# First projection of a hybrid encoder step: nine pairs of tiles as seven half-size block products

## The chip, the core and the metric

The kernel runs on one core of a Trainium2 chip. The metric is the time of one execution on the device, in microseconds. TensorE multiplies matrices, VectorE, ScalarE and GpSimd do the elementwise work, SyncE issues nearly all transfers between memory and the core's on-chip memory. Each engine runs its own instructions in order; semaphores tie them together.

## The reference

One layer of a streaming encoder is run on 1024 prompt tokens and 32 sample tokens with the same weights. The part that the change touches is the first line and what reads its result:

```python
z = x @ w["w_in"]            # (1056 x 1024) @ (1024 x 6416)
gq, gk, gv, gr, ga, sq, sk, sv, mq, gl = jnp.split(z, SPLIT_AT, axis=-1)
log_a = log_sigmoid(ga @ w["w_gla_a2"] + w["b_gla_a"]) / GLA_TAU
o_a, gla_s = gla_chunked(gq, gk, gv, log_a, gla_s0, ...)   # branch A: recurrence over tokens
q, k = partial_rope(sq, pos), partial_rope(sk, pos)        # branch B: first 16 of 64 dims turned
o_c = mem_attention(mq, mem_k, mem_v)                      # branch C; keys from mem_prompt @ w_mem_kv
g_a, g_b, g_c = jnp.split(sigmoid(gl + w["b_gate"]), 3, axis=-1)
mix = (g_a * y_a + g_b * y_b + g_c * y_c) @ w["w_o"]
x = layer_norm(ALPHA * x + mix);  x = layer_norm(ALPHA * x + conv_ffn(x))
```

All is float32. A product is made of three matmuls on rounded halves: `hi @ hi + hi @ lo + lo @ hi`.

## The kernel before

Activations lie transposed: 128 channels on the partitions, tokens along the free dimension, 1058 columns (1024 prompt, a gap of 2, 32 sample), in three slices of 352, 352 and 354 (`GROUPS`). x arrives as 9 tiles of 128 rows, TensorE turns each (`x_turn`, L1057), ScalarE rounds it to `act_hi` (L1581), VectorE makes the rest, `act_lo` (L2124).

**A dense tile** is 128 columns of `w_in`. SyncE loads it to `w_raw` (`cols`, L564, issued on L562), ScalarE makes `w_hi` (`split_hi`, L1565), VectorE `w_lo` (`split_lo`, L2113). There are two slots; a slot is loaded again when its split is done. TensorE then does three slices (`proj_slice`, L1044) of 8 x 3 matmuls, alternating between banks 0 and 1 of the accumulator. ScalarE copies each slice into `z` (`proj_out`, L1571) or, for a merge gate's tile, into a staging buffer `gate_st` (`gate_out`, L1621), from which SyncE writes it to scratch memory (`gates_scratch`, L619). The count `proj_free` of those copies lets TensorE into a bank again.

**The order of the program.** (1) 16 dense tiles fill `z` (the four inputs of the recurrence); the narrow `ga` (16 columns, L1608 to L1610 and L2147) stands between tiles 14 and 15. (2) The recurrence: 8 steps of 128 tokens and one of 32 (`gla_tile` on each engine). Each step has six places for a slice of a dense tile (`gate_slice`, L1162), so 18 tiles stand beside it: 16 gate tiles (0 to 15), then two of `sq`. (3) Eight more dense tiles (`sk`, `sv`, `sq` 2 and 3, four `mq`), written to the `z` rows that the recurrence has left. After the fourth of them TensorE turns the 256 memory rows (`mem_rows_turn`, L1185), loaded by SyncE on L642 and L643. Beside the last four stand the four tiles of the memory keys (`mem_tile`). Rotary embedding needs rows of `z` moved to other partitions: per tile, four transfers of 8 partitions each (`rope_rows`, L658), a product with `sin` on VectorE (L2218), with `cos` on GpSimd (L897), and a sum (L2222). (4) Attention over window and memory, 8 more gate tiles, the merge of the branches, `w_o`, the first norm. (5) The up-projection of the FFN. (6) The down-projection and the second norm.

**The up-projection is already in block form.** A pair of tiles (256 columns) is cut into 2 x 2 blocks: 512 + 512 input channels, 128 + 128 output columns, and the tokens of a slice in two halves of 256 or 274 (`HALF`). Seven products of half size replace eight. A product is 4 x 3 matmuls (`block_product`, L1438, its matmuls L1462); both token slices follow each other within a product, so a pair has 7 x 2 x 12 = 168 matmuls. GpSimd makes four sums of weight blocks, ScalarE rounds the seven operands (L1886), VectorE makes their low parts (L2449). ScalarE copies four results out of the accumulator (`snap_out`, L1934), VectorE adds three (`combine`, L2492). Sums of x blocks are made once.

## Time and profile before

| | us |
|---|---|
| median of 3 runs | 1777.21 (1776.03 to 1777.63) |
| the profiled execution | 1777.36 |
| its span in the trace | 1775.5 |
| mean granted TensorE clock in it | 0.996 of full speed |

The profile is one execution, with the start and the duration of every instruction on every engine, and what released an engine that had been idle. Copies out of the accumulator mark the progress of the program: the last slice of the second dense tile is copied at 45.0 us, the copies of `ga` begin at 199.44, that of the last slice beside the recurrence is at 476.00. The chain enters the steady part of the up-projection at 1093.46.

### The profile page before, as it was taken

To read this page: it belongs to the slowest core of one execution; us is meant where nothing else is said; L and a number is where in the kernel's file an instruction comes from. 1 tells how busy PE (TensorE), PEld (TensorE's weight loads), DVE (VectorE), ACT (ScalarE), POOL (GpSimd) and SP (SyncE) were. 2 spreads that over 40 slices of the span, in tenths; PEclk is the share of its full clock that TensorE was granted. 3 is DMA by queue.
4 is the path that set the end of the run, shared out by engine and by line. 5 is a ranking of instruction groups with operands and counts; after the bars stand their busy time and mean duration, and the time that the engine had idled before them with its cause. 6 is when DMAs were issued, how large, how long until landed. Compare 5 with 4: busy or idle time off the path is not lost.

```text
span 1775.5 us, 31156 instructions
## 1 busy us (share of the span) xinstructions
PE 1750.6 (99%) x11872; PEld 1695.5 (95%) x11872; DVE 1001.9 (56%) x1379; ACT 716.7 (40%) x1272; POOL 231.7 (13%) x324
## 2 busy tenths in 40 slices
PE   8999999999999999999999999999999999999997
PEld 7999999999999799989998889999999999999997
DVE  3111165555242766657656688777777677554464
ACT  3222244343222555554332245545444454433342
POOL 0000000000020200000000014333333331002011
PEclk9999999999999999999999999999999999999999
DMA  5111122122422411124454232222222223885662
GB/s 176 48 47 36 46 67 84 60 88 66 118 58 72 128 50 48 33 75 136 133 181 143 82 91 74 72 86 81 79 77 72 72 72 107 260 266 165 214 228 73
DMA packets 181451, 180.30 MB, mean 102 GB/s; under 512 B 21021, under 2 KB 149086, under 8 KB 181374
## 3 DMA queue, kind: packets, MB, share of 16 engines
q1 hardware_dynamic: 179518, 173.24, 32.1%
q0 software_dynamic: 1856, 5.99, 0.9%
q8 instruction: 53, 0.87, 0.2%
q14 instruction: 24, 0.20, 0.0%
HBM read 143.08 MB, written 35.53 MB: 101 GB/s over the span
## 4 chain that ended last, share of the span: by engine, by line
PE 94%; DVE 3%; issue 1%; ACT 1%; DMA 1%; POOL 0%; SPq 0%; ACTq 0%; POOLq 0%; DVEq 0%
PE banks L1462 24%; PE banks L1028 19%; PE banks L1029 18%; PE banks L1030 18%; PE banks L1419 5%; PE banks L1256 1%; PE banks L1273 1%; PE banks L1236 1%; PE banks L1268 1%; PE banks L1241 1%; DMA x_rows<-in_x_prompt 0%; PE banks L1136 0%; PE banks L1148 0%; PE banks L1142 0%; PE banks L1430 0%
## 5 line engine op out<-in xcount | busy, mean ns | idle before, releaser
L1028 PE MATMUL banks<-act_hi,w_hi 128*128 128x352 f32 (+1 forms) x1200 | 395.9, 330 | 1.3 <-DVE act_lo L2124 1.3
L1030 PE MATMUL banks<-act_hi,w_lo 128*128 128x352 f32 (+1 forms) x1200 | 390.1, 325 | 0.0
L1029 PE MATMUL banks<-act_lo,w_hi 128*128 128x352 f32 (+1 forms) x1200 | 389.9, 325 | 0.0
L2113 DVE TENSOR_TENSOR w_lo<-w_raw,w_hi 128x1024 fp32r<-128x1024 f32 x70 | 87.3, 1248 | 317.4 <-ACT w_hi L1565 317.4
L1028 PEld LDWEIGHTS banks<-act_hi,w_hi 128*128 128x128 f32 x1200 | 226.9, 189 | 6.1 <-issue 2.4
L1462 PE MATMUL banks<-x_free_r,a_hi 128*128 128x256 f32 x1232 | 226.8, 282 | 0.8 <-DVE a_lo L2449 0.5
L1029 PEld LDWEIGHTS banks<-act_lo,w_hi 128*128 128x128 f32 x1200 | 226.8, 189 | 0.4
L1030 PEld LDWEIGHTS banks<-act_hi,w_lo 128*128 128x128 f32 x1200 | 226.7, 189 | 0.0
L1462 PEld LDWEIGHTS banks<-x_free_r,a_hi 128*128 128x128 f32 x1232 | 190.1, 188 | 1.3 <-DVE x_free_r L2475 0.7
L1462 PE MATMUL banks<-xs_hi,a_hi 128*128 128x274 f32 x616 | 178.8, 290 | 1.7 <-DVE xs_lo L2475 1.0
L1462 PE MATMUL banks<-xs_lo,a_hi 128*128 128x274 f32 x616 | 178.4, 290 | 0.0
L1462 PE MATMUL banks<-xs_hi,a_lo 128*128 128x274 f32 x616 | 178.3, 289 | 0.0
L1462 PE MATMUL banks<-x_free_r,a_lo 128*128 128x256 f32 x616 | 173.4, 281 | 0.0
L1029 PE MATMUL banks<-h_lo,w_hi 128*128 128x384 f32 (+1 forms) x448 | 147.3, 329 | 0.0
L1028 PE MATMUL banks<-h_hi,w_hi 128*128 128x384 f32 (+1 forms) x448 | 146.8, 328 | 0.0
L1030 PE MATMUL banks<-h_hi,w_lo 128*128 128x384 f32 (+1 forms) x448 | 146.5, 327 | 0.0
L1571 ACT ACTIVATE z<-banks 128x352 f32<-128x352 f32 (+3 forms) x78 | 36.4, 466 | 239.3 <-PE banks L1030 239.3
L2605 DVE TENSOR_TENSOR w_lo<-w_raw,w_hi 128x1024 fp32r<-128x1024 f32 x56 | 68.5, 1224 | 93.7 <-ACT w_hi L2044 93.3
L1462 PEld LDWEIGHTS banks<-xs_hi,a_hi 128*128 128x128 f32 x616 | 116.4, 189 | 2.3 <-DVE xs_lo L2475 1.5
L1462 PEld LDWEIGHTS banks<-xs_lo,a_hi 128*128 128x128 f32 x616 | 116.7, 190 | 0.0
L1462 PEld LDWEIGHTS banks<-x_free_r,a_lo 128*128 128x128 f32 x616 | 116.6, 189 | 0.0
L1462 PEld LDWEIGHTS banks<-xs_hi,a_lo 128*128 128x128 f32 x616 | 116.3, 189 | 0.0
(314 smaller groups left out, 3335.2 us busy)
## 6 DMA issues: line engine op xcount, KB each, us to landing
w_raw<-in_w_down SPq DMA_DIRECT2D x112, 256.0 KB, 3.4
w_raw<-in_w_in SPq DMA_DIRECT2D x100, 256.0 KB, 3.3
gate_in<-gates_scratch SPq DMA_DIRECT2D x24, 529.0 KB, 3.8
h_keep<-conv SPq DMA_DIRECT2D x22, 530.0 KB, 2.7
w_raw<-in_w_up SPq DMA_DIRECT2D x44, 256.0 KB, 3.8
x_free<-in_w_up SPq DMA_DIRECT2D x44, 256.0 KB, 3.6
h_raw<-h_keep SPq DMA_DIRECT2D x22, 384.0 KB, 5.1
gates_scratch<-gate_st SPq DMA_DIRECT2D x32, 176.0 KB, 1.9
```

Source lines behind the costliest of these rows:

```text
L1028: pe.matmul(out, hi, b_hi, start=start, stop=False)
L1029: pe.matmul(out, hi, b_lo, start=False, stop=False)
L1030: return pe.matmul(out, lo, b_hi, start=False, stop=stop)
L1236: last = pe.matmul(psum[0:w, 2 + r, h * 256:h * 256 + nk], qs[b][rows_, 2 * u + h, 0:w], keys[rows_, 0:nk], start=True, stop=True)
L1241: last = pe.matmul(out, mqs[b][:, h, 0:w], mkT[mem][:, h, :], start=True, stop=True)
L1256: last = pe.transpose(pair8(4)[0:n, 2 * h + s, 0:w], prob[par][0:w, h, s * P:s * P + n], ident[0:w, 0:w])
L1268: last = pe.matmul(bank4(6)[64 * r:64 * r + 64, h, 0:w], pair_[s][0:n, 64 * r:64 * r + 64], prob_T[0:n, 2 * (2 * r + h) + s, 0:w], start=( ...
L1419: last = pe.matmul(bank(b + half), x[:, k, c:c + P], w[:, place, 512 * half:512 * half + 512], start=k == 0 and n_ == 0, stop=k == KD - 1 ...
L1462: last = pe.matmul(out, a[j][:, k, :], x[s][j][:, k, :], start=fresh and k == 0 and n_ == 0, stop=k == 3 and n_ == 2, skip_group_check=True)
L1571: act.activation(z[:, bass.ds(chunk, 1), c:c + w].rearrange("p k c -> p (k c)"), bank(par)[:, 0:w], ACT.Copy).then_inc(q.proj_free, 1)
L2113: dve.tensor_tensor(dst[:, :, :], w_raw[slot][:, :, :], src[:, :, :].bitcast(F32), ALU.subtract).then_inc(q.w_split_lo, 1)
L2605: dve.tensor_tensor(d_lo[i][:, :, :], d_raw[i][:, :, :], d_hi[i][:, :, :].bitcast(F32), ALU.subtract)\
```

## The change

The first projection gets the block form for nine pairs, 18 of its tiles. In the code of after, `zd` are the staging buffers of two dense tiles, `zt_*` the sums of x blocks and their halves, `za_*` those of the weights, `zu` the staging buffers of a pair, `xf` an unrounded copy of x.

- x is copied once more out of the accumulator to `xf`: five of the nine tiles by ScalarE, three full ones and the one of 32 columns by VectorE.
- Tiles 0 and 1 stay dense. Then come seven pairs (tiles 2 to 15 of `z`) and two pairs of gate tiles (12 to 15). VectorE makes the sums of x and of the weights. Results go to `zu` and from there to scratch memory, since the sums, `zt_*`, lie where `z` is.
- Then gate tile 10, `ga`, gate tile 11, all dense. The constants of `ga` and of the recurrence are loaded here, and `z` is read back in two transfers, 256 columns and the other 802.
- The 18 places beside the recurrence hold `sq` 0 and 1, `sk`, `sv`, `sq` 2 and 3, two `mq`, and gates 0 to 9. All go by the staging buffers to scratch memory.
- After the recurrence two `mq` tiles are left; the memory rows are turned in the second, and the four tiles of memory keys follow in a row.
- Rotary embedding works on the 16 turned rows of each half tile, packed: 30 transfers read them from scratch memory, VectorE does the arithmetic for four tiles at once, 10 transfers write them back. `sq`, `sk`, `sv` and `mq` come back from scratch memory too.

```diff
+        def z_load(n):
+            par = n % 2
+            col = C_GQ + (2 + 2 * n) * P if n < 7 else C_GL + (12 + 2 * (n - 7)) * P
+            for half in range(2):
...
+        def z_keep(n):
+            to = Z_KEEP + 2 + 2 * n if n < 7 else 12 + 2 * (n - 7)
+            for s in range(2):
+                sp.wait_ge(q.combined[s], 3 * n + 3)
+                sp.wait_ge(q.snapped[s], 4 * n + 4)
+            sp.wait_ge(q.z_stored, z_stored_count(n - 1))
+            sp.dma_start(gates[to:to + 2].rearrange("r p c -> p r c"), zu[n % 2][:, :, :]).then_inc(q.z_stored, 16)
...
+        for s in range(2):
+            sp.wait_ge(q.prod_mm[s], ZA)
+        sp.dma_start(wga[:, :, :], w_in[:, :, C_GA:C_GA + RANK]).then_inc(q.gla_consts, 16)
...
+        def z_again(lo, hi):
+            sp.dma_start(z[:, :, lo:hi], gates[Z_KEEP:Z_KEEP + 16, :, lo:hi].rearrange("r p c -> p r c")).then_inc(q.z_back, 16)
+        z_again(0, 2 * P)
+        z_keep(NZ - 1)
...
+        fill_load(0)
+        staged_store(PS_Z, 0, 10)
+        staged_store(PS_Z, 1, 10)
+        sp.wait_ge(q.z_back, 16)
+        z_again(2 * P, TT)
...
-            sp.wait_ge(gate_stored[s], 16 * 16)
+            sp.wait_ge(gate_stored[s], 16 * 20)
         sp.wait_ge(q.st_state, 32)
+        def turned_rows(dst, row, landed):
+            for h in range(2):
+                to, of = ROPE_DIM * h, SWA_HD * h
+                sp.dma_start(dst[0][0][dst[1] + to:dst[1] + to + 16, :], gates[A_KEEP + row, of:of + 16, :]).then_inc(landed, 16)
+                for a, b in ((0, 8), (8, 0)):
+                    sp.dma_start(dst[0][1][dst[1] + to + a:dst[1] + to + a + 8, :], gates[A_KEEP + row, of + b:of + b + 8, :]).then_inc(landed, 16)
+        turned_rows((k_rot, 0), 8, rot_landed[0])
         sp.dma_start(cos[:, :], I["c_cos"]).then_inc(q.att_consts, 16)
         sp.dma_start(sin[:, :], I["c_sin"]).then_inc(q.att_consts, 16)
-        for j in range(2):
-            swa_q(T_ATT // 2 + 2, j, 2 + j)
+        for row in range(4):
+            turned_rows((rot, 32 * row), row, rot_landed[1])
+        sp.dma_start(z[:, 0:6, 6 * P:TT], gates[A_KEEP:A_KEEP + 6, :, 6 * P:TT].rearrange("r p c -> p r c")).then_inc(q.z_back, 16)
...
         sp.dma_start(mem_rows[0][:, :], I["mem_prompt"][0, 0:P, :]).then_inc(q.mem_in, 16)
...
+        def z_product(n, par, s, j):
...
+            for k in range(4):
+                for n_, (a, v) in enumerate(((za_hi, x_hi), (za_hi, x_lo), (za_lo, x_hi))):
+                    last = pe.matmul(bank(b)[:, 0:w], a[j][:, k, :], v[:, k, :], start=fresh and k == 0 and n_ == 0, ...)
...
-        for t in range(9):
-            c, w = tok(t)
...
+        x_out(1, xf)
+        x_out(2, xf)
...
+            if t >= 5:
+                dve.tensor_copy(xf[:, :, c:c + w], x_bank(t)[:, :, 0:w]).then_inc(q.x_lo_done, 1)
...
-        for n_ in range(2, 10):
-            if n_ < 6:
-                turn_, slot = (T_ATT + n_) // 2, n_ % 2
+        for n_ in range(2):
+            tile_start(T_MQ // 2, n_)
...
+        for i in range(4):
+            mem_tile(T_MK // 2 + i // 2, i % 2, 0, i)
```

**ScalarE's list in the first pair.** Here `zd` is the copy of a dense slice, `zt_hi` the rounding of an x sum, `za_hi` that of a weight block, and the first `zu` the copy of the pair's first product. Before, at the second dense tile:

```order
L1571 ACTIVATE z<-banks 128x354 [waits proj_done]
L1565 ACTIVATE w_hi_59<-w_raw_57 128x1024 [waits w_landed0]
L1571 ACTIVATE z<-banks 128x352 [waits proj_done] x2
L1571 ACTIVATE z<-banks 128x354 [waits proj_done]
L1565 ACTIVATE w_hi_60<-w_raw_58 128x1024 [waits w_landed1]
L1597 ACTIVATE prm<-banks 128x289 [waits prm_turned]
```

After, at the same tile:

```order
L1813 ACTIVATE za_hi_111<-z_sum_105 128x512 [waits a_summed]
L1813 ACTIVATE za_hi_114<-z_sum_105 128x512 [waits a_summed]
L1785 ACTIVATE zd_103<-banks 128x352 [waits proj_done]
L1791 ACTIVATE zt_hi_82<-zt_sum_98 128x1096 [waits x_summed]
L1791 ACTIVATE zt_hi_83<-zt_sum_99 128x1096 [waits x_summed]
L1785 ACTIVATE zd_103<-banks 128x354 [waits proj_done]
L1813 ACTIVATE za_hi_113<-z_sum_104 128x512 [waits proj_done,a_summed]
L1813 ACTIVATE za_hi_115<-w_raw_58 128x512 [waits proj_done,w_landed1]
L1827 ACTIVATE zu_106<-banks 128x256 [waits x_summed,prod_mm0]
L1827 ACTIVATE zu_106<-banks 128x256 [waits prod_mm0] x2
```

Between the slices of the second dense tile and behind them there are now six roundings, and the product's copy stands behind them all.

**SyncE's list between the pairs and the recurrence, after.** The rows before the first of these are loads of gate tile 10's and 11's weights; `L617` is the load of a dense tile.

```order
L699 DMA wga<-in_w_in 128x8x16 [waits prod_mm1,prod_mm0]
L700 DMA causal<-in_c_causal 128x128
L702 DMA wa_raw<-in_w_gla_a 16x512 x6
L704 DMA wa_raw<-in_b_gla_a 1x512 x2
L708 DMA z<-gates_scratch 128x16x256
L677 DMA gates_scratch<-zu_106 128x2x1058 [waits snapped1,combined1,z_stored,snapped0,combined0]
L617 DMA w_raw_57<-in_w_in 128x8x64 [waits w_split_lo]
L617 DMA w_raw_57<-in_w_in 128x8x64
L726 DMA gates_scratch<-gate_st_153 128x352 [waits proj_free]
L726 DMA gates_scratch<-gate_st_154 128x352 [waits proj_free]
L708 DMA z<-gates_scratch 128x16x802 [waits z_back]
```

The constants wait for the last product of the pairs, and the next tile's weights stand behind them, behind the first read of `z` and behind the store of the last pair. Before, the constants stood at the start of the program (L598 to L603), and this place held weight loads alone.

**SyncE's list at the end of the recurrence.** Before (the waits on the stores are the same semaphores as after):

```order
L638 DMA cos<-in_c_cos 128x1058 [waits gate_stored1,gate_stored2,gate_stored0,st_state,ds_mm,gla_out]
L639 DMA sin<-in_c_sin 128x1058
L562 DMA w_raw_57<-in_w_in 128x8x64 [waits w_split_lo]
L562 DMA w_raw_57<-in_w_in 128x8x64
L562 DMA w_raw_58<-in_w_in 128x8x64 [waits w_split_lo]
L562 DMA w_raw_58<-in_w_in 128x8x64
L642 DMA mem_rows_125<-in_mem_prompt 128x1024
L643 DMA mem_rows_126<-in_mem_prompt 128x1024
L644 DMA mask<-in_c_mask 128x256
L645 DMA mask_first<-in_c_mask_first 128x256
L658 DMA rot_127<-z 8x1058 [waits proj_free,rot_cleared]
L658 DMA rot_127<-z 8x1058 x3
```

After, where `k_rot` and `rot` hold the packed rows:

```order
L782 DMA k_rot_183<-gates_scratch 16x1058 [waits gate_stored1,gate_stored2,gate_stored0,st_state,ds_mm,gla_out]
L784 DMA k_rot_184<-gates_scratch 8x1058 x2
L782 DMA k_rot_183<-gates_scratch 16x1058
L784 DMA k_rot_184<-gates_scratch 8x1058 x2
L787 DMA cos<-in_c_cos 128x1058
L788 DMA sin<-in_c_sin 128x1058
L782 DMA rot_181<-gates_scratch 16x1058
L784 DMA rot_182<-gates_scratch 8x1058 x2
```

and, after six more groups of three such transfers:

```order
L782 DMA rot_181<-gates_scratch 16x1058
L784 DMA rot_182<-gates_scratch 8x1058 x2
L791 DMA z<-gates_scratch 128x6x290
L792 DMA z<-gates_scratch 128x290
L793 DMA kpad<-gates_scratch 128x1058
L794 DMA mem_rows_179<-in_mem_prompt 128x1024
L795 DMA mem_rows_180<-in_mem_prompt 128x1024
L796 DMA mask<-in_c_mask 128x256
L797 DMA mask_first<-in_c_mask_first 128x256
```

The memory rows and the masks stood behind two constants and four weight loads; now they stand behind 30 row transfers, two constants and three reads.

## Rows read from the trace of the kernel before

**Rows 1.** Page, part 1: each engine's busy time (share of the span) and instructions.
```profile
PE 1750.6 (99%) x11872; PEld 1695.5 (95%) x11872; DVE 1001.9 (56%) x1379; ACT 716.7 (40%) x1272; POOL 231.7 (13%) x324
```

**Rows 2.** Page, part 4, the chain's shares; waits of TensorE: total, times, longest.
```profile
PE 94%; DVE 3%; issue 1%; ACT 1%; DMA 1%; POOL 0%; SPq 0%; ACTq 0%; POOLq 0%; DVEq 0%
...
PE banks L1064 <- DMA x_rows<-in_x_prompt: 3.6, 2, 3.1
```

**Rows 3.** Timeline of ScalarE, dense loop: start, duration, operation [idle before <-releaser].
```profile
57.02 0.47 ACT L1571 ACTIVATE z<-banks 128x354 f32 x1 [3.41 <-PE banks L1030]
...
68.68 0.47 ACT L1571 ACTIVATE z<-banks 128x354 f32 x1 [3.42 <-PE banks L1030]
```

**Rows 4.** Chain that ended last, by time: its longest piece (start, duration, count).
```profile
1093.46 408.10 PE banks L1462 x3312
```

**Rows 5.** Timelines of VectorE, then TensorE, where the third dense slice begins.
```profile
26.39 1.21 DVE L2113 TENSOR_TENSOR w_lo<-w_raw,w_hi 128x1024 fp32r<-128x1024 f32 x1
27.52 1.55 DVE L2124 TENSOR_TENSOR act_lo<-banks,act_hi 128x1024 fp32r<-128x1024 f32 x2
...
29.13 0.44 PE L1028 MATMUL banks<-act_hi,w_hi 128*128 128x354 f32 x1 [0.37 <-DVE act_lo L2124]
```

**Rows 6.** Groups by form (total, mean ns); last, two operations of VectorE's timeline.
```profile
L2492 DVE TENSOR_TENSOR u<-banks,snap 128x256 f32<-128x256 f32 x44 | 18.1, 412 | 2.1 <-PE banks L1462 2.1
L2605 DVE TENSOR_TENSOR d_lo<-d_raw,d_hi 128x1024 fp32r<-128x1024 f32 x10 | 12.2, 1221 | 5.2 <-ACT d_hi L2044 5.1
...
L1886 ACT ACTIVATE a_hi<-w_raw 128x512 fp32r<-128x512 f32 x33 | 20.7, 627 | 21.0 <-PE banks L1462 18.2 <-PE banks L1430 2.8
...
250.37 0.69 DVE L2169 TENSOR_TENSOR e_t<-b_s 128x512 f32<-128x512 f32 x1
250.97 0.69 DVE L2171 SCALAR_TENSOR_TENSOR q_dec<-z,e_p 128x512 f32<-128x512 f32 x1
```

**Rows 7.** SyncE by tile: count, issue time min/median/max in ns, first and last start.
```profile
L658 SPq DMA_DIRECT2D rot<-z x20: 624/625/797, 482.3 to 530.0; - x20
...
L601 SPq DMA_DIRECT2D wa_raw<-in_w_gla_a x6: 419/420/2779, 16.9 to 21.6; - x6
```

**Rows 8.** DMA issues: count, KB each, median us from issue to landing.
```profile
gates_scratch<-gate_st SPq DMA_DIRECT2D x32, 176.0 KB, 1.9
...
mem_rows<-in_mem_prompt SPq DMA_DIRECT2D x2, 512.0 KB, 5.1
```

**Rows 9.** Windows: busy PE, PEld, DVE, ACT, POOL, granted clock, DMA share, GB/s.
```profile
10.00:13.00 3.00, 0.00 (x0) 0.00 (x0) 2.94 (x3) 1.99 (x3) 0.00 (x0) 0.91 1.01 404
13.00:14.50 1.50, 1.41 (x7) 1.41 (x8) 0.54 (x1) 0.00 (x0) 0.00 (x0) 0.50 1.11 332
15.20:16.00 0.80, 0.80 (x5) 0.80 (x4) 0.00 (x0) 0.80 (x1) 0.00 (x0) 0.57 1.09 392
46.00:190.00 144.00, 144.00 (x891) 144.00 (x890) 15.93 (x13) 29.33 (x51) 0.00 (x0) 1.00 0.17 45
1480.00:1560.00 80.00, 80.00 (x514) 80.00 (x514) 49.10 (x52) 37.35 (x47) 5.05 (x12) 1.00 0.62 198
```

**Rows 10.** Timelines of ScalarE, then SyncE, around the end of the recurrence.
```profile
476.00 0.47 ACT L1571 ACTIVATE z<-banks 128x354 f32<-128x354 f32 x1 [3.10 <-PE banks L1030]
...
473.63 0.34 SPq L638 DMA_DIRECT2D cos<-in_c_cos  x1
...
479.73 1.03 SPq L642 DMA_DIRECT2D mem_rows<-in_mem_prompt  x1
```

**Rows 11.** TensorE by tile: the transposes of the memory rows.
```profile
L1185 PE MATMUL banks<-ident,mem_rows x16: 271/273/273, 514.6 to 520.1; 128*128 128x128 f32 x16
```

**Rows 12.** Timelines of ScalarE and VectorE: the three steps of one `ga` slice.
```profile
199.44 0.45 ACT L1608 ACTIVATE ga_T<-banks 32x352 fp32r<-32x352 f32 x1 [1.17 <-PE banks L1097]
...
200.47 0.45 ACT L1610 ACTIVATE ga_T<-banks 32x352 fp32r<-32x352 f32 x1 [0.58 <-DVE ga_T L2147]
...
199.92 0.52 DVE L2147 TENSOR_TENSOR ga_T<-banks,ga_T 32x352 fp32r<-32x352 f32 x1 [0.40 <-ACT ga_T L1608]
```

784 lines of the change are left out of this document (558 added, 226 removed).

## The prediction

> **What bounds the kernel now.** I read the page first: TensorE is busy for 1750.6 of 1775.5 us, VectorE and ScalarE for about half [rows 1], and the chain that ended last is 94% TensorE [rows 2]. So any column of a matmul that goes away is time won, and any wait that TensorE gets is time lost, one for one. The list of who waited for whom gives TensorE under 10 us of waits in the whole span, most of it for the first transfers, so nothing that the other engines do today is paid for. Two unit prices follow. A dense tile (72 matmuls of 352 or 354 columns) takes 11.66 us: the copies of the third slice of two tiles in a row start at 57.02 and 68.68 [rows 3]. A pair of tiles as seven block products (168 matmuls of 256 or 274 columns) is what the up-projection already does: 3312 of them in 408.10 us [rows 4] are 19.71 pairs of 20.70 us, 123 ns a matmul.
>
> **The change part by part.**
>
> *The products.* Nine pairs leave the dense form: 9 x (2 x 11.66 - 20.70) = 23.6 us off the path. The count of tiles stays 42 up to the first scores (2 + 18 + 2 alone, 18 beside the recurrence, 2 for the memory queries). In the steady loop each pair asks VectorE for 11 operations of 512 and 6 of about 265 elements. One of 512 lasts 0.69 and the next begins 0.60 after it when they stand in a row [rows 6], so I take 0.63; one of 1024 lasts 1.21 and lets the next in after 1.13 [rows 5], so 1.19. That is 11 x 0.63 + 6 x 0.41 = 9.4 us, and less on ScalarE, inside 20.7 us. The loads of 1.05 MB and the store of 1.08 MB a pair need 7 us of transfer at 320 GB/s. Cost of those: nothing, the products cover them; without cover 9.4 us a pair.
>
> *The start.* VectorE now also copies four of the tiles into `xf`, three ahead of what the third dense slice waits for, and ScalarE copies five. Before, VectorE's last two `act_lo` operations began at 27.52 and TensorE went on at 29.13 after a wait of 0.37 [rows 5]. Now two full copies of 1.13 us pitch stand between, less what was idle: the third slice starts at about 31.0. Cost 1.9 us (1 to 3).
>
> *The first pair.* VectorE is free of x at 31.3. In front of the fourth weight sum its list holds 12 operations of 1024 or 1096 elements and 8 of 512: 12 x 1.19 + 8 x 0.63 = 19.3 us, so 50.6. ScalarE has the split that waits for this sum in front of two slice copies, two x-sum copies, two splits and only then the copy of the first product (0.55 + 2 x 0.4 + 2 x 1.05 + 2 x 0.5 + 0.4 = 4.9 us; a split of 512 elements lasts 0.63 [rows 6], a tenth less in a row, a slice's copy 0.47 [rows 3]), and 0.3 for the hand-overs: 55.8. TensorE ends the six dense slices at 46.8 and three products later, at 51.1, needs that copy: a wait of 4.7 us. The same list gives two more, 0.4 and 1.5 us, where products 6 wait for `combined` behind splits. Sum 6.6 us (4 to 8).
>
> *From the pairs to the recurrence.* Let T be the end of the ninth pair. Ten small transfers (issue 0.46 us each, rows of `wa_raw` [rows 7]) start only at T, so the constants land at T + 6.6, and ScalarE, which waits for them, frees the first dense slice at T + 8.9; TensorE asked at T + 7.8: 1.2 us. Behind them on the queue stand 2.1 MB (z, 256 columns), 1.1 MB (last store) and 0.5 MB (weights). At full occupation this trace moved 198/0.62 = 320 GB/s, 45/0.17 = 265 for 512-byte pieces, and 404 for rows of 4 KB [rows 9]. With 320 the weights land at T + 4.6 + 11.6 + 2 = T + 18.2. ScalarE's split stands ahead of its `ga_T` copies and VectorE's ahead of its own: 1.05 + 1.22 + 1.4 for the three steps of a slice [rows 12] gives T + 21.9, while TensorE wants the bank for the third `ga` slice at T + 18.0: 3.9 us. The remaining 6.6 MB then need 20.5 us, the second tile of weights lands at about T + 39.5 and ScalarE, stuck behind its split, is free for the first gate of the recurrence at T + 43.7; TensorE needs it at T + 44.9. At 265 GB/s this would be a wait of 4. I take 0.5. The 2.8 MB fetched in the eighth recurrence step delay one weight split by 1 to 2 us against 1.6 of slack: 0.5. Sum 6.1 us (3 to 13).
>
> *From the recurrence to the scores.* Let G be the end of the recurrence's last fill; before, its copy stands at 476.00 [rows 10]. Before, SyncE issued `cos` at 473.63 and the memory rows at 479.73 [rows 10], and TensorE first used them at 514.6 [rows 11]: 35 us of cover. Now the fills are stored, and SyncE must see the last store land first: G + 0.5 + 0.4 + 1.9 [rows 8] = G + 2.8. Ahead of `mem_rows` stand 30 row transfers: 10 of 16 partitions at 0.46 us and 20 of 8 partitions at 0.67 (issue 0.42 and 0.625 plus the gap [rows 7]), 18.0 us, then `cos` and `sin`, 0.8. So the first large transfer goes at G + 21.6. Up to the masks it is 2.9 MB, 8.4 us at 345 GB/s (between 320 and 404, since half of it is rows of 4 KB), and 2 us to land: G + 32. And only two dense tiles are left before the memory products, with the turn of the memory rows after the first slice of the second: G + 11.7 + 3.9 = G + 15.5. TensorE waits 16.5 us. Bounds: all 30 at 0.46 and 404 GB/s give 11; 8-partition issues of 0.8 (the longest row) and 320 GB/s give 20. The four memory tiles now stand in a row, 2.5 us each, and two of them have only one buffer's lead for load and split: 1.5 us more (0 to 3). Rope itself, the `cos` product and the kpad copy were behind cover and stay so. Sum 18.0 us.
>
> The row shows 0.625 us for the issue of an 8-partition transfer and 0.42 for one of 16 [rows 7]. The Trainium skill, DMA: Bandwidth & Descriptors, section Why a DMA increments its semaphore by 16 and not by 1, says that a transfer runs on the largest number of engines up to 16 that divides its outermost dimensions, and that the issuer itself writes the missing increments when it is fewer; the trace agrees with that as a reason for the difference.
>
> *The clock.* After a wait of 3.1 us at the start the granted clock stood at 0.50, the lower level of 1.2 GHz, until about 15.9 [rows 9]: 2.8 us at half speed cost 1.4. Two of the new waits are longer. I add 1.3 for each, 2.6 (0 to 4). The Trainium skill, TensorE: Matmul & The Clock Gate, section Part 1: The HAM clock gate, says that an idle array is throttled to half and is given full speed back after sustained work. By it the long wait costs this; the trace agrees.
>
> **Sum.** -23.6 + 1.9 + 6.6 + 6.1 + 18.0 + 2.6 = +11.6 us. The profiled execution took 1777.4 us (span 1775.5), within 0.2 of the median 1777.2; so 1789.0 us, 0.7% slower. The bounds added up are -4 and +25; a measurement tells 0.2% (3.6 us) from no change.
>
> **The rivals.** *The memory rows are covered after all* (the other side). If the 30 issues overlap with the wait for the last store, or the row transfers and the large reads run side by side at 400 GB/s, the wait at G + 15.5 shrinks to 3 or less with no cold clock: 1789.0 - 13.5 - 1.3 = 1774.2; with the first pair and T at their lower bounds (2.6 and 3.1 less) 1768.5. It decides where the large reads start before G + 6. For it: mask and memory rows landed in 5 us before. Against: all sit on one queue, in order, behind a wait. *The scratch reload is the bound*: 9.8 MB in pieces of 1 to 3 KB at 265 GB/s or less, with fills' stores behind it, adds 4 at the recurrence's first step and 3 at the third `ga` slice: 1796. For: ScalarE stands in order behind weight splits. Against: 320 seen with mixed pieces. *The pairs run slower than in the up-projection*, since VectorE now makes the sums itself: one late `combined` of 0.8 us in each of 9 pairs is 7 us: 1796. Against: VectorE carries more there (the conv and GpSimd beside it).
>
> **Chances.** Forecast 0.55 (1782 to 1796); memory rows covered 0.28, of which 0.16 ends faster by over 0.2% and 0.12 within; reload 0.12; slow pairs 0.05. So faster 0.16, same 0.14 (0.02 of it from the forecast's low end), slower 0.70. Range for 8 in 10: 1773 to 1799.
>
> **What would show it.** Dense pairs gone: 1512 matmuls of the L1462 shape in nine stretches of 20.7 us. TensorE idle before the third product's stretch at 51 us, before the third `ga` slice, and, longest of all, before the first transpose of `mem_rows`, put down to a transfer; on SyncE 18 us of row issues just before. If that last wait is under 5 us, the forecast is wrong in its largest term; if the nine pairs take more than 190 us with no wait named above, the gain is.

## The result, and the profile after

The changed kernel takes 1787.89 us in the median of 5 executions (1785.18 to 1790.10), beside 1777.21 for the kernel before: a ratio of 1.0061, 95% interval 1.0046 to 1.0076. It is slower, by 10.7 us, where 1789.0 was forecast. The profiled execution is the slowest of the five, 1790.1 us with a span of 1788.0; the distances below are measured in it, against the profiled execution of before (1777.4, span 1775.5).

The page of the changed kernel, part 1 and the chain's shares, which answer to [rows 1, 2]:

```profile
PE 1736.7 (97%) x12088; PEld 1679.5 (94%) x12088; DVE 1079.6 (60%) x1529; ACT 749.9 (42%) x1348; POOL 219.2 (12%) x319
...
PE 89%; DVE 5%; DMA 2%; ACT 2%; issue 1%; SPq 1%; POOL 0%; ACTq 0%; POOLq 0%; DVEq 0%
```

TensorE is busy 13.9 us less, and the span is 12.5 us longer. The chain's TensorE share fell from 94 to 89%. The list of TensorE's waits in the changed kernel (engine, tile and line, releaser: total us, times, longest) says on what:

```profile
PE banks L1386 <- DMA mask_first<-in_c_mask_first: 14.9, 1, 14.9
PE banks L1302 <- ACT ga_T L1922: 4.8, 1, 4.8
PE banks L1171 <- DVE act_lo L2422: 3.6, 2, 2.6
...
PE banks L1228 <- ACT zu L1827: 2.3, 1, 2.3
PE banks L1228 <- DVE zu L2473: 1.6, 1, 1.6
PE banks L1171 <- DVE w_lo L2411: 1.2, 1, 1.2
...
PE banks L1171 <- ACT gate_st L1912: 0.9, 1, 0.9
```

In the order of the program: `act_lo` and `w_lo` are the start, the two `zu` are the first pair, `ga_T` and `gate_st` stand between the pairs and the recurrence, and `mask_first` is the wait before the memory rows are transposed. Two pieces of the chain of the changed kernel, in order of time (start, duration, count):

```profile
75.85 166.96 PE banks L1228 x1356
...
1106.53 408.12 PE banks L1659 x3312
```

And the milestones between them: on TensorE's timeline the first product and the first scores,

```profile
50.92 0.28 PE L1228 MATMUL banks<-act_hi,za_hi 128*128 128x256 f32 x1
...
595.74 1.14 PE L1433 MATMUL banks<-ks,qs 64*128 64x256 f32 x8
```

the first scores of the kernel before,

```profile
582.81 1.14 PE L1236 MATMUL banks<-ks,qs 64*128 64x256 f32 x8
```

and on ScalarE's the copy of the last fill's last slice:

```profile
541.50 0.47 ACT L1912 ACTIVATE gate_st<-banks 128x354 f32<-128x354 f32 x1 [3.03 <-PE banks L1173]
```

The long stretch of pairs runs without a stop until 242.81, 123 ns a matmul or 20.7 us a pair, just as the up-projection [rows 4] does. So the gain of the products is there in full, and all that was lost lies in four places. The start of the steady part moved from 1093.46 [rows 4] to 1106.53. By milestones (before: six dense slices end at 45.00, the last fill's copy is at 476.00 [rows 10], the first scores begin at 582.81):

| stretch | cost measured, us | forecast, us |
|---|---|---|
| start, to the first product | +5.9 | +1.9 |
| first pair (50.92 to 77.3, against 20.7) | +5.7 | +6.6 |
| end of pairs (242.81) to the last fill's copy | +7.6 | +6.1 and 1.3 for the clock |
| last fill's copy to the first scores | +17.4 | +18.0 and 1.3 for the clock |
| nine pairs | -23.6 | -23.6 |
| sum at the first scores | +13.0 | +11.6 |

For the third line, before's stretch is 476.00 - 45.00 less 12 dense tiles of 11.66 (the changed kernel makes 18 tiles as pairs ahead of it, and before had six of those behind the last fill): 291.1, against 298.7. For the fourth it is 106.8 less those six, 36.8, against 54.2.

Two of these costs differ from trace to trace, and the trace shown is of the slowest execution. Experiments 1, 2, 3, 5, 6 and 9 below leave everything up to the second pair as it is; there the start and the first pair together cost 8.2 to 10.4 us, against 11.6 here and 8.5 forecast. Experiments 3, 4, 6, 7, 8 and 10 leave everything behind the last fill as it is; there the fourth cost is 13.6 to 17.2.

The longest wait can be read from SyncE's timeline of the changed kernel (start, duration, transfer, count):

```profile
544.01 0.34 SPq L782 DMA_DIRECT2D k_rot<-gates_scratch  x1
...
554.86 0.65 SPq L784 DMA_DIRECT2D rot<-gates_scratch  x2
...
557.04 0.53 SPq L794 DMA_DIRECT2D mem_rows<-in_mem_prompt  x1
...
558.77 0.52 SPq L797 DMA_DIRECT2D mask_first<-in_c_mask_first  x1
```

and from TensorE's, with the idle time before the operation:

```profile
571.93 1.33 PE L1386 MATMUL banks<-ident,mem_rows 128*128 128x128 f32 x5 [14.91 <-DMA mask_first<-in_c_mask_first]
```

With G for the copy at 541.50: the row transfers begin at G + 2.5 and TensorE stops at G + 15.5, both where the prediction has them (2.8 and 15.5). But the rows and the two constants leave the queue after 11.5 us, not 18.8, and the last mask, issued at 558.77, lands 13.2 us later, not 2 us behind 8.4 us of transfer. The two errors nearly cancel. Windows of the changed kernel show what happened in those 13 us (busy PE, PEld, DVE, ACT, POOL, granted clock, DMA share, GB/s):

```profile
550.00:553.00 3.00, 3.00 (x21) 3.00 (x20) 0.45 (x1) 0.00 (x0) 0.00 (x0) 1.00 0.86 167
553.00:556.00 3.00, 3.00 (x20) 3.00 (x19) 2.90 (x3) 0.47 (x1) 0.00 (x0) 1.00 0.68 120
556.00:560.00 4.00, 1.01 (x7) 0.72 (x5) 0.33 (x1) 0.00 (x0) 0.00 (x0) 0.97 0.97 125
...
565.00:570.00 5.00, 0.00 (x0) 0.00 (x0) 2.18 (x2) 0.00 (x0) 0.00 (x0) 0.50 1.04 396
```

From 550 to 560 the DMA engines are 68 to 97% busy and move only 120 to 167 GB/s; the large reads behind the rows move 396. The last column but two is the clock: 0.50 while TensorE stands.

### The profile page after: what moved, and what is told of

Read it like the earlier page. It is cut to its first block, busy times and chain, and to the rows that moved or that the text cites. A ratio compares the mean times of both kernels' runs of the same rounds, so it can differ in the third digit from the quotient of the medians.

```text
span 1788.0 us, 31834 instructions
## 1 busy us (share of the span) xinstructions
PE 1736.7 (97%) x12088; PEld 1679.5 (94%) x12088; DVE 1079.6 (60%) x1529; ACT 749.9 (42%) x1348; POOL 219.2 (12%) x319
## 4 chain that ended last, share of the span: by engine, by line
PE 89%; DVE 5%; DMA 2%; ACT 2%; issue 1%; SPq 1%; POOL 0%; ACTq 0%; POOLq 0%; DVEq 0%
PE banks L1659 23%; PE banks L1171 14%; PE banks L1172 14%; PE banks L1173 13%; PE banks L1228 10%; PE banks L1616 5%; PE banks L1453 1%; PE banks L1470 1%; PE banks L1433 1%; PE banks L1465 1%; PE banks L1438 1%; DMA mask_first<-in_c_mask_first 1%; DMA w_raw<-in_w_in 1%; PE banks L1343 0%; PE banks L1355 0%
## 5 line engine op out<-in xcount | busy, mean ns | idle before, releaser
L1171 PE MATMUL banks<-act_hi,w_hi 128*128 128x352 f32 (+1 forms) x768 | 258.0, 336 | 5.6 <-DVE act_lo L2422 3.6
L1172 PE MATMUL banks<-act_lo,w_hi 128*128 128x352 f32 (+1 forms) x768 | 251.8, 328 | 0.0
L1173 PE MATMUL banks<-act_hi,w_lo 128*128 128x352 f32 (+1 forms) x768 | 251.8, 328 | 0.0
L1171 PEld LDWEIGHTS banks<-act_hi,w_hi 128*128 128x128 f32 x768 | 147.2, 192 | 9.8 <-DVE act_lo L2422 4.2
L1172 PEld LDWEIGHTS banks<-act_lo,w_hi 128*128 128x128 f32 x768 | 147.0, 191 | 0.4
L1173 PEld LDWEIGHTS banks<-act_hi,w_lo 128*128 128x128 f32 x768 | 147.0, 191 | 0.0
L2411 DVE TENSOR_TENSOR w_lo<-w_raw,w_hi 128x1024 fp32r<-128x1024 f32 x52 | 63.7, 1225 | 118.3 <-ACT w_hi L1762 118.3
L3021 DVE TENSOR_TENSOR w_lo<-w_raw,w_hi 128x1024 fp32r<-128x1024 f32 x56 | 68.4, 1223 | 91.8 <-ACT w_hi L2342 91.6
L2865 DVE TENSOR_TENSOR a_lo<-a_sum,a_hi 128x512 fp32r<-128x512 f32 x86 | 83.6, 972 | 40.7 <-ACT a_hi L2184 39.5
```

The lines of the kernel that those rows point to most:

```text
L1171: pe.matmul(out, hi, b_hi, start=start, stop=False)
L1172: pe.matmul(out, hi, b_lo, start=False, stop=False)
L1173: return pe.matmul(out, lo, b_hi, start=False, stop=stop)
L2411: dve.tensor_tensor(dst[:, :, :], w_raw[slot][:, :, :], src[:, :, :].bitcast(F32), ALU.subtract).then_inc(q.w_split_lo, 1)
L2865: dve.tensor_tensor(a_lo[j][:, :, :], src, a_hi[j][:, :, :].bitcast(F32), ALU.subtract).then_inc(q.a_lo_done, 1)
L3021: dve.tensor_tensor(d_lo[i][:, :, :], d_raw[i][:, :, :], d_hi[i][:, :, :].bitcast(F32), ALU.subtract)\
```

## The experiments

My theory after the result: each of the four places is a matter of order. A step sits in an in-order list behind something that it does not need. The rivals: that each wait is transfer time, which another order only shifts; and that behind each wait the next one is already due, so that a repair of one gains little. All kernels below are the changed kernel with one edit, unless said otherwise; times are medians, and gains are against 1787.9.

**1. The memory rows ahead of the row transfers.**

```diff
+        sp.dma_start(mem_rows[0][:, :], I["mem_prompt"][0, 0:P, :]).then_inc(q.mem_in, 16)
...
+        sp.dma_start(mask_first[:, :], I["c_mask_first"]).then_inc(q.mem_in, 16)
         turned_rows((k_rot, 0), 8, rot_landed[0])
```

> The changed kernel, with the four loads of the memory rows and the masks issued ahead of the 30 row transfers of rope instead of behind them; nothing else moves. Theory (the wait of 14.9 us before the first transpose of the memory rows is their place behind 30 issues and three reads): that wait goes to 0, since the rows land about 8 us after the last store. But the weights of the first key tile keep their place behind the rows, and ScalarE's split of them stands ahead of its copy of the last query tile's first slice; in the changed kernel it waited for them until 575.9. So TensorE meets a new wait of about 7 us at the third slice of that tile, and the gain is 8 us and perhaps 1 of clock: about 1779. Rival 1 (the bytes are what takes the time, not the order: 2.9 MB at 340 GB/s must pass in any order): the wait shrinks by 2 us at most, 1786. Rival 2 (the memory rows were the only thing late): the whole 14.9 and the cold clock go, 1771.

Measured: 1784.14 (1779.92 to 1785.27), ratio 1.0035 [1.0021, 1.0049]: 3.8 us gained of 14.9. In this kernel's list of TensorE's waits:

```profile
PE banks L1171 <- ACT z L1768: 12.4, 1, 12.4
```

and ScalarE's timeline:

```profile
570.54 1.06 ACT L1762 ACTIVATE w_hi<-w_raw 128x1024 fp32r<-128x1024 f32 x1 [19.98 <-DMA w_raw<-in_w_mem_kv]
```

The wait for `mask_first` is gone, and one of 12.4 stands a dense tile later. The next thing TensorE needs are the keys' weights, and they still sit behind the 30 rows. ScalarE waits 20 us for them, with the copy that frees TensorE's bank behind it in its list. In the changed kernel that split waited already (at 575.87, idle 22.24), hidden by the wait in front.

**2. The keys' weights ahead as well.**

```diff
+        mem_tile(T_MK // 2, 0, 0, 0)
+        mem_tile(T_MK // 2, 1, 0, 1)
         turned_rows((k_rot, 0), 8, rot_landed[0])
```

> As the run before, and the loads of the first two key tiles stand ahead of the row transfers too. Theory: ScalarE's split is no longer late, so the last query tile runs through; but VectorE's low part of the first key tile stands behind rope in its list, and rope ends some 24 us after the last store, so TensorE waits for it about 3 us, and about 4 for the third key tile, whose load stands behind rope's write-backs. Gain against the changed kernel 14.9 + 2 of clock - 7, about 10: 1778. Rival (rope has slack, as it had before the change): 17 us, 1771. Rival (ScalarE's split was not what held the copies): the same as the run before.

Measured: 1785.0 (1783.56 to 1787.21), ratio 1.0048 [1.0031, 1.0064]. No gain over the first. This kernel's list of TensorE's waits:

```profile
PE banks L1171 <- DVE mem_lo L2651: 13.4, 1, 13.4
```

and ScalarE's timeline:

```profile
572.70 1.94 ACT L1990 ACTIVATE mem_hi<-banks 128x1024 fp32r<-128x1024 f32 x2 [14.12 <-DMA kpad<-k_rot]
```

and the end of VectorE's turn of the keys, and their write-back on SyncE:

```profile
560.52 1.25 DVE L2643 TENSOR_TENSOR k_rot<-k_rot,k_rot 32x1058 f32<-32x1058 f32 x1
...
569.65 1.28 SPq L807 DMA_DIRECT2D kpad<-k_rot  x2
```

This one I had overlooked. `mem_hi` lies where `k_rot` lay, so ScalarE may write it only when the turned keys are written back to `kpad`. VectorE has turned them at 561.8, but SyncE issues the write-back only at 569.65: it stands behind the wait for the large reads of `z` and `kpad`. So a shared buffer hands SyncE's order on to ScalarE.

**3. The recurrence's first weights ahead of `z` and the last store.**

```diff
-        z_again(0, 2 * P)
-        z_keep(NZ - 1)
         fill_load(0)
+        z_again(0, 2 * P)
+        z_keep(NZ - 1)
         staged_store(PS_Z, 0, 10)
```

> The changed kernel, with the load of the first tile beside the recurrence issued ahead of the first read of z and of the last pair's store, instead of behind them. Theory (the wait of 4.8 us at the third ga slice is ScalarE standing in front of a weight load that lies behind 3.2 MB): the load lands about 5 us after the constants instead of 14, the 4.8 us and the half-speed stretch behind it (about 2 us) go, and the reads of z end 1.5 us later, which the recurrence does not feel: 1788 - 6.5 = 1781.5. Rival (z is the bound: what the weights gain, the first step of the recurrence gives back, since its read of z ends later): no change, 1788 within 1.

Measured: 1786.68 (1784.59 to 1788.39), ratio 1.0053 [1.0036, 1.0070]. The split of the weights now starts at 255.05, but the wait for `ga_T` is still 5.1. ScalarE's row:

```profile
264.45 0.45 ACT L1922 ACTIVATE ga_T<-banks 32x352 fp32r<-32x352 f32 x1 [6.72 <-DVE ga_T L2566]
```

The releaser is now VectorE. It stands on its wait for the last pair's store, ahead of the clearing of `att`, and the weight split and its part of `ga_T` come behind. Again a second wait of the same length, one list further on.

**4. The first pair in another order.** The sums for products 3 and 4 go ahead of the second x sums on VectorE, and the combination of the first products ahead of the second half's sums.

```diff
         z_x_sums(1)
-        z_low(0, 0, 2)
-        z_sums34(0, 0)
...
         z_low(0, 0, 1)
+        z_low(0, 0, 2)
+        z_sums34(0, 0)
```

> The changed kernel, with VectorE's last two weight sums of the first pair ahead of the second four x sums, and one combine of the first pair ahead of the second pair's last sums. Theory (ScalarE's copy of the first product is late because it stands behind splits that wait for those weight sums, and TensorE waits 2.3 us for it and 1.6 for the combine): the copy now waits only for the last x sum, at 52.9 us instead of 57.1, the first wait goes, the second falls to 0.6, and with them a stretch at a lower clock of about 1 us: 1788 - 4.3 = 1783.7. Rival (the copy is bound by the x sums themselves, since the staging buffer lies on xf and the sums end 1.9 us later now): the first wait stays at 2 us, 1787.

Measured: 1788.45 (1785.03 to 1790.23), ratio 1.0058 [1.0042, 1.0075]. The copy of the first product is in time, and nothing is gained. TensorE's wait in this kernel:

```profile
PE banks L1228 <- DVE zu L2473: 5.3, 2, 4.7
```

and its timeline of ScalarE:

```profile
59.87 2.12 ACT L1791 ACTIVATE zt_hi<-zt_sum 128x1096 fp32r<-128x1096 f32 x2 [4.52 <-DMA gates_scratch<-zd]
```

ScalarE waits for the store of the dense tiles, which on SyncE stands behind a load that waits for the x sums. TensorE's wait for ScalarE became one for VectorE.

**5. The row transfers made small.** The 30 transfers stay, each with 64 of its 1058 columns, and the rope works on as many, so the kernel leaves out the rope of the other columns. This tells issue time from transfer time.

```diff
-                sp.dma_start(dst[0][0][dst[1] + to:dst[1] + to + 16, :], gates[A_KEEP + row, of:of + 16, :]).then_inc(landed, 16)
+                sp.dma_start(dst[0][0][dst[1] + to:dst[1] + to + 16, 0:64], gates[A_KEEP + row, of:of + 16, 0:64]).then_inc(landed, 16)
```

> The changed kernel, with rope's 30 row transfers and 10 write-backs cut to 64 of 1058 columns, and its arithmetic too: as many issues in the same places, a sixteenth of the bytes (the rope of the other columns is left out). It parts the price of the rows into issues and bytes. Theory of the prediction (the wait before the memory rows is the time that SyncE needs to issue 30 transfers, and the queue empties as fast as it is filled): the last large load is still issued 18 us after the last slice's copy and lands at most 2 us earlier; the wait stays at 12.5 to 15, time 1786 to 1788. Rival (the traces so far: all 33 issues took 11.5 us, and the transfer engines were 70 to 100% occupied behind them, at 120 to 170 GB/s, while the row pieces passed): the bytes of the rows hold up what stands behind them, the large loads land 10 us after their issue instead of 14, and the wait falls to 9 to 10, time 1782.

Measured: 1780.73 (1779.58 to 1783.15), ratio 1.0025 [1.0014, 1.0036]. The row of this kernel's TensorE timeline:

```profile
562.60 1.97 PE L1386 MATMUL banks<-ident,mem_rows 128*128 128x128 f32 x8 [9.24 <-DMA mask_first<-in_c_mask_first]
```

and two of its windows, the columns as above:

```profile
550.00:553.00 3.00, 3.00 (x20) 3.00 (x19) 0.15 (x2) 0.00 (x0) 0.00 (x0) 1.00 0.10 10
556.00:560.00 4.00, 0.00 (x0) 0.00 (x0) 0.00 (x0) 0.00 (x0) 0.00 (x0) 0.50 1.04 412
```

The issues take 11.5 us as before (540.36 to 551.88). TensorE goes on 7.4 us after the last mask's issue (555.17) instead of 13.2. The wait is 9.2 instead of 14.9, so 5.7 us would be the rows' own transfer, during which the DMA engines are busy at a third of their rate. One pair of traces can't give this size. In the six experiments that leave this block as it is (3, 4, 6, 7, 8, 10) the wait is 11.2 to 15.0, and TensorE goes on 9.3 to 13.2 us after the last mask's issue, with the same transfers in the same order. Experiment 5's 7.4 lies below all of them, so the rival that the rows cost transfer time, not issue alone, holds; the size is between 2 and 6 us of the wait (the medians differ by 7.2, with the clock behind the wait in it). Why the same transfers land so differently is not shown.

**6. Experiment 3 and the clearing of `att` behind both splits.**

```diff
-        dve.wait_ge(q.z_stored, z_stored_count(NZ - 1))
-        dve.memset(att[:, :, :], 0.0)
         split_lo(2, 0)
...
         split_lo(2, 1)
+        dve.wait_ge(q.z_stored, z_stored_count(NZ - 1))
+        dve.memset(att[:, :, :], 0.0)
```

> The kernel of e3, and VectorE's wait for the last pair's store, with the clearing of the attention buffer behind it, moved from ahead of the ga slices to behind them. In e3 the weights were no longer late, but VectorE's first low part of ga came only at 263.9, released by that wait, and TensorE's wait stayed at 5.1. Theory (two waits stood one behind the other at the same place, and either alone holds the bank): now the 5.1 us go and the half-speed stretch behind them (262 to 270, 3 us) with them: e3's 1786.7 - 7.5 = 1779. Rival (the wait comes back at the first step of the recurrence, since z is read back later than the tiles before it now end): 1784.

Measured: 1783.20 (1779.45 to 1788.40), ratio 1.0038 [1.0027, 1.0048], a gain of 4.7 where 9 was expected. The wait for `ga_T` is gone, and the granted clock between 251 and 276 us is 1.00. What came behind, in this kernel's list of waits:

```profile
PE banks L1171 <- ACT gate_st L1912: 4.2, 2, 2.9
```

and on ScalarE's timeline:

```profile
280.02 0.47 ACT L1912 ACTIVATE gate_st<-banks 128x354 f32<-128x354 f32 x1 [10.12 <-DMA gates_scratch<-gate_st]
```

The last store of gate tile 10 stands behind the second read of `z`, as it did in the changed kernel; the tiles before it now end earlier, and its staging buffer comes back too late for them.

**7. Experiment 4 and the dense tiles' store ahead of the load that waits.**

```diff
+        z_keep_dense(1)
         sp.wait_ge(q.x_summed, XS0)
         z_load(1)
-        z_keep_dense(1)
```

> The kernel of e4, and the store of the second dense tile ahead of the load of the second pair's weights. In e4 the copy of the first product came in time (51.3 instead of 57.1), but the sums of the second slice then waited 4.5 us for that store, whose buffer they overwrite, and TensorE 4.7 us for the combine behind them. Theory: the store now lands at about 54 instead of 59.9, this wait shrinks to 0.5, and the stretch at 0.8 of the clock goes: e4's 1788.4 - 5.5 = 1783. Rival (a third wait behind it: the weights of pair 1, loaded 1 us later): the gain is under 2 us.

Measured: 1781.59 (1778.65 to 1782.63), ratio 1.0023 [1.0013, 1.0033], a gain of 6.3. The first pair's waits in this kernel:

```profile
PE banks L1228 <- DVE zu L2473: 1.2, 2, 0.6
```

From 3.9 us to 1.2. In this trace the first pair takes 22.3 us, against 24.1 to 28.0 in experiments 1, 2, 3, 5, 6 and 9. Experiment 4 alone gave nothing, and the two together pay; the store alone was not run.

**8. The copies of x into `xf` on GpSimd**, as a sum of the two halves, off VectorE and ScalarE.

```diff
+            pool.tensor_tensor(xf[:, :, c:c + w], act_hi[:, :, c:c + w].bitcast(F32), act_lo[:, :, c:c + w].bitcast(F32),
+                               ALU.add).then_inc(q.xf_done, 1)
```

> The changed kernel, with the unrounded copy of x made by GpSimd as act_hi + act_lo, instead of by ScalarE and VectorE from the accumulator. Theory (the start lost 6.1 us: ScalarE's and VectorE's nine copies delay the first slices, TensorE waits 2.6 + 0.9 + 1.2 us and runs at half speed twice): the start comes back to that of the kernel before, the first product begins at 45 to 46 instead of 50.9, and since VectorE reaches the sums 4.5 us earlier the first pair keeps its waits: 1788 - 5 = 1783. Rival (GpSimd working beside VectorE slows it: act_lo takes 1.5 to 2 us instead of 1.22, as a_lo in the up-projection takes 0.97 to 1.18 against 0.68 alone): the start gains under 2 us, 1786 or more.

Measured: 1788.40 (1785.52 to 1789.67), ratio 1.0059 [1.0042, 1.0076]. No gain. VectorE's timeline in this kernel:

```profile
13.12 2.60 DVE L2406 TENSOR_TENSOR w_lo<-w_raw,w_hi 128x1024 fp32r<-128x1024 f32 x1
...
33.92 3.34 DVE L2426 TENSOR_TENSOR zt_sum<-xf,zt_sum 128x1024 f32<-128x1024 f32 x1
```

In the changed kernel these take 1.21 and 1.22. GpSimd's additions stretch those of VectorE's operations beside them that have both inputs in SBUF; `act_lo`, which reads one of its two from the accumulator, keeps 1.21 to 1.23 beside them. The expected first product at 45 to 46 came at 48.00, and the first pair is late again (a wait of 6.9 for `zu`).

**9. The whole block of the memory rows.** Experiment 2, with `k_rot` in a place of its own, so that ScalarE's wait ahead of `mem_hi` goes; `mem_lo` between the two rope steps on VectorE; two more key tiles' loads ahead of the write-backs.

```diff
-    k_rot = [at(f"k_rot{i}", [2 * ROPE_DIM, TT], F32, offset=MEM_AT + align(TT * 4) * i) for i in range(2)]
+    k_rot = [at(f"k_rot{i}", [2 * ROPE_DIM, TT], F32, offset=o) for i, o in enumerate((align(QS_AT + 2 * align(TT * 4)), align(Z_AT + 8 * TT * 4)))]
...
-        act.wait_ge(rot_landed[0], 16 * 8)
```

> The kernel of e2 (memory rows, masks and the first two key tiles ahead of the row transfers), with the three waits gone that e2 showed behind it: the small turned buffers lie elsewhere, so that ScalarE need not wait for their write-back before it rounds the memory rows (14.1 us idle in e2); VectorE does the first key tile's low part ahead of rope, and the memory rows' and the second key tile's between its two parts; and the loads of key tiles 3 and 4 stand ahead of rope's write-backs. Theory (the wait of 14.9 us is a stack of four: rows, ScalarE's weights, ScalarE's buffer, VectorE's and SyncE's order; each alone gave 2 to 5 us since the next lay just behind it): TensorE waits less than 3 us between the recurrence and the scores, no half-speed stretch is left there, the first scores come 36.8 + 3 us after the last slice's copy instead of 54.2: 1788 - 14 = 1774. Rival (rope itself is the bound, since its rows land 22 us after the last store and its write-backs take 5 us of issues and land last): the scores wait for the write-back instead, 5 to 8 us, and the time is 1779.

Measured: 1778.93 (1777.00 to 1781.77), ratio 1.0012 [1.0003, 1.0022], a gain of 9.0 where 14 was expected. The single wait of 14.9 became four small ones, 7.0 us together where less than 3 was expected (this kernel's list, `w_lo` being two of them):

```profile
PE banks L1171 <- DVE w_lo L2410: 3.1, 2, 1.6
...
PE banks L1171 <- DVE mem_lo L2649: 2.5, 1, 2.5
...
PE banks L1422 <- ACT mk_rows L1997: 1.4, 1, 1.4
```

The time is the rival's 1779, but not by its mechanism: none of these waits is one for the write-backs. Other traces of the old order in this block had waits of 11.2 to 15.0, so the gain is read from the medians.

**10. Three copies into `xf` behind the last `act_lo`**, so that the third dense slice is not held up.

```diff
-            if t >= 5:
-                dve.tensor_copy(xf[:, :, c:c + w], x_bank(t)[:, :, 0:w]).then_inc(q.x_lo_done, 1)
+            if t == 5:
+                x_copy(t)
...
+        for t in range(6, 9):
+            x_copy(t)
```

> The changed kernel, with VectorE's copies of the seventh and eighth x tile behind its last act_lo instead of between them. Theory (two copies of 1.13 us stand ahead of what the third dense slice waits for): that slice begins at 31.1 instead of 33.4, the wait of 2.6 falls to 0.4, as before the change, and the half-speed stretch at 34 to 37, which the traces show after it in some executions, no longer comes: between 2.3 and 4 us off, about 1785, and the first product begins between 45 and 47 in place of 46.8 to 50.9. Rival (the first pair's lists are the bound: VectorE reaches the sums at the same time): the start gains and the first pair waits that much longer, 1788.

Measured: 1787.45 (1785.41 to 1788.22), ratio 1.0060 [1.0044, 1.0075]. TensorE reaches the first product at 45.92, and then waits 6.1 us for `zu` instead of 2.3. With the lists of the first pair as they are, a quicker start only lengthens the wait behind it. What shortens it is their order and the store's, as experiment 7 shows.

**11. Experiments 6, 7, 9 and 10 together**, and the second read of `z` behind the fills' first stores.

```diff
-        sp.wait_ge(q.z_back, 16)
-        z_again(2 * P, TT)
...
+        sp.wait_ge(q.z_back, 16)
+        z_again(2 * P, TT)
```

> All orders together: the memory block of e9, the first pair and store of e7, the late x copies of e10, and between the pairs and the recurrence the order of e6 with one more step (gate tile 10's last store and the recurrence's second weight tile ahead of the large read of z, since e6 had ScalarE idle 10.1 us for that store and TensorE 2.9 for it). Theory (all that the change lost is order, and the gain of 24 us stands behind it): 1788 less 14 (memory block), 6.3 (e7's), 8 (e6's 4.7 and 3 more) and 2.3 (start), so 1757, 1.1% under the kernel before. Rival (order moves the waits but transfers set the end: 3 + 5 MB around the recurrence have to pass): not under 1768.

Measured: 1767.89 (1766.78 to 1771.10), ratio 0.9954 [0.9940, 0.9968]: 9.2 us faster than the kernel before, 20 us faster than the change. The gains of its parts, 4.7, 6.3, 9.0 and 0.4, sum to 20.4 and give 1767.5, so they add up, and the further step, for which I had counted 3 us, shows no gain of its own. The 1757 that I had expected counted gains that the single runs had not shown. The time stands at the rival's bound, 1768; whether transfers set it is not shown, since what is left in this kernel's list are waits for VectorE and ScalarE:

```profile
PE banks L1171 <- DVE w_lo L2410: 5.6, 3, 3.4
...
PE banks L1228 <- DVE za_lo L2460: 1.9, 1, 1.9
```

**12. The last key tiles earlier still**: the third key tile's load among the groups of row transfers, the fourth's ahead of a wait.

```diff
             turned_rows((rot, 32 * row), row, rot_landed[1])
+            if row == 2:
+                mem_tile(T_MK // 2 + 1, 0, 0, 2)
```

> The kernel of e11, with the load of the third key tile after the third of the four groups of rope's rows instead of behind the reads of z and kpad, and that of the fourth ahead of SyncE's wait for these reads. In e11 ScalarE stood idle 7.0 and 3.6 us for these two weights and TensorE waited 5.0 us for the low parts. Theory (their place in the queue is what is late, as for the memory rows before): the weights land at about 550 and 558 instead of 560 and 564.7, the 5.0 us fall to 2 or less, and the time is 1767.9 - 3 = 1765. Rival (rope's write-backs are the bound behind them: GpSimd stages the first scores only at 568.2 in e11, when z is back, and the scores begin at 570.1): the time goes from one wait to the next, and 1767.9 stays within 1.

Measured: 1769.41 (1765.12 to 1774.40), ratio 0.9962 [0.9951, 0.9972]; it can't be told from the eleventh. The key tiles' waits shrank (`w_lo` 2.1), and this came for them, in the list of this kernel's waits:

```profile
PE banks L1434 <- POOL mqs L1055: 2.7, 1, 2.7
```

and the row of GpSimd's timeline:

```profile
565.17 0.60 POOL L1047 COPY qs<-z 128x512 f32<-128x512 f32 x1 [45.27 <-DMA z<-rot]
```

The turned queries, the last user of the row transfers, are now late themselves. Whether the transfers set this, or once more the order (the write-backs stand behind two waits of SyncE), was not tested. The eight executions spread over 9.3 us, too wide to price it.

## Why the prediction was right, point by point

*What bounds the kernel.* Right. TensorE was the bound without slack, and every wait that it got showed in the time. One reading was wrong, without weight for the sum: the waits that the list of the kernel before names for TensorE are 13.5 us, not under 10, and 6.3 of them are for the first transfers.

*The products.* Right: 20.69 us a pair, -23.6 us. The rival of slow pairs (VectorE makes the sums here) is out: the long stretch has no wait. Experiment 11 shows the gain is real: the kernel is 9.2 us faster in all, and most of the other 14.4 stand in its list as waits that before did not have (12.8 us).

*The start.* The term was right; what was missing is the clock, for which the prediction gave this stretch nothing. In experiments 2, 5, 6 and 7, which had full clock from 16 to 21 us, the third dense slice begins at 30.8 to 31.2, where 31.0 was forecast. In experiments 2 and 7, which kept it, the first product begins 1.8 and 2.1 us later than before, against 1.9. With the same instructions up to there, the changed kernel's profiled execution cost 5.9. Its third slice begins at 33.40, behind a longer stretch at half speed, and a second such stretch follows the wait of 2.6 us for `act_lo`. Windows, columns as above, of the changed kernel:

```profile
16.00:21.00 5.00, 5.00 (x24) 4.92 (x23) 2.23 (x2) 1.94 (x2) 0.00 (x0) 0.56 0.73 197
...
34.00:38.00 4.00, 4.00 (x17) 4.00 (x17) 3.96 (x4) 2.12 (x2) 0.00 (x0) 0.57 0.00 0
```

and of experiment 2:

```profile
16.00:21.00 5.00, 4.57 (x33) 4.26 (x31) 2.55 (x3) 3.80 (x5) 0.00 (x0) 1.00 0.70 180
...
34.00:38.00 4.00, 4.00 (x27) 4.00 (x26) 4.00 (x5) 3.58 (x6) 0.00 (x0) 1.00 0.34 135
```

They go with first products at 50.92 and 46.78; experiment 5, with full clock in the first window and 0.69 in the second, has 49.51. The stretch behind the wait of 2.6 us is in seven of the nine traces that have this wait (all but experiments 2 and 7), and in none of the four that don't (8, 10, 11 and 12). The profiled execution of the change is 2.2 us above its median. The executions of all kernels that have this start scatter over 3.6 to 9 us where those of before scatter over 1.6 to 3.2; but experiments 11 and 12, without the wait, scatter over 4.3 and 9.3, so the start is not all of it.

*The first pair.* Right in what waits for what, and near in size, 5.7 against 6.6: waits of 2.3 and 1.6 us, and 1.8 of lower clock after them, which was not in the term. The first wait is smaller than the 4.7 forecast because TensorE came 4 us late to it; in experiment 2, where it came on time (46.78), the wait is 3.8. Two readings of it were too simple. Experiment 4 shows that ScalarE's place behind the splits was only the first of two bounds, with the store behind it; experiment 10 that what the start gains the first pair's wait takes, so start and first pair are not two independent terms.

*From the pairs to the recurrence.* Right: the weights landed 19.3 us after the end of the pairs (18.2 forecast), the wait for `ga_T` is 4.8 (3.9), the one ahead of it, for the copy of the first dense slice, 0.9 (1.2); the two of 0.5 behind them did not come. Experiment 6 shows the part that was not in the working: VectorE's own wait for the same store. The rival of a reload at 265 GB/s is out: the windows from 251 to 266 us move 289 to 345, the one below 415, and no wait stands at the recurrence's first step.

*From the recurrence to the scores.* Total right (17.4, and 13.6 to 17.2 in the other traces, against 19.3 with the clock), inner sizes wrong, and in opposite directions: issues 7.3 us too long, landing 6.0 too short. That the total came out is luck. The step "20 of 8 partitions at 0.67" failed. SyncE's issues of `rot`, and of the fills' stores, in the changed kernel (count, min/median/max in ns, first and last start):

```profile
L784 SPq DMA_DIRECT2D rot<-gates_scratch x16: 295/311/326, 547.5 to 555.2; - x16
L782 SPq DMA_DIRECT2D rot<-gates_scratch x8: 315/316/425, 547.0 to 554.5; - x8
L812 SPq DMA_DIRECT2D z<-rot x8: 587/589/632, 568.7 to 573.2; - x8
...
L726 SPq DMA_DIRECT2D gates_scratch<-gate_st x60: 332/333/8052, 256.7 to 542.0; - x60
```

L784 is the 8-partition transfer, L782 the 16-partition one, and they issue in the same time. The 0.625 of [rows 7] belongs to `rot<-z`, 8 partitions, which has both ends on the chip; so has `z<-rot`, 16 partitions and 0.589. The source alone is not it: the stores of `gate_st` leave the chip and take 0.333. I had put down to the partitions what goes with both ends being on the chip. So what the Trainium skill says of the missing increments (DMA: Bandwidth & Descriptors, section Why a DMA increments its semaphore by 16 and not by 1) does not hold as the reason for longer issues: the trace doesn't agree. The step "8.4 us at 345 GB/s and 2 us to land" failed too, by about the same amount, since it let the rows cost issue time only; experiment 5 puts 2 to 6 us on their transfer. The rival on the other side, that the rows are covered, is out, but what it named as decisive was right: the time at which the large reads start. Experiment 9 moves that, with three orders behind it, and 9 us come back.

*The clock.* Too small in sum: 2.6 was forecast for two long waits, and the profiled execution lost about 4 in the start and 1.8 in the first pair besides. Where it was counted it was near. The window before the transposes has 0.50 during the wait, as has this window of the changed kernel, behind the wait for `ga_T`:

```profile
266.00:269.00 3.00, 3.00 (x12) 1.61 (x11) 0.52 (x1) 0.45 (x1) 0.00 (x0) 0.50 1.03 415
```

TensorE's timeline there:

```profile
265.55 0.50 PE L1302 MATMUL banks<-act_hi,wga_split 128*32 128x354 f32 x1 [4.77 <-ACT ga_T L1922]
```

The first matmuls behind it take 0.50 us, those from 269.66 on 0.32 to 0.33. Some 4 us at half speed cost about 2, against the 1.3 forecast for each long wait.

*The sum.* The bounds of the terms add up to -4.6 and +27.4, not to the -4 and +25 of the prediction. The +13.0 measured by milestones and the +10.7 of the medians lie inside either.

What stays open: why the clock from 16 to 21 and from 34 to 38 us, and the landing of the memory rows, differ between executions of the same instructions. No run here separates it.
